# Positive part of the stick groups moved to ScalarE, and transposes copied before exponentials and masks in the dilated steps

## The reference

```python
# nsa_mixer: compressed, selected and window attention, softmax with slopes
# dilated_mixer: three groups of keys (distances up to 128, every 4th up to 512,
# every 16th up to 2048), softmax each, merged by their denominators
# stick_breaking_mixer:
z = jnp.einsum('bqhd,bshd->bhqs', qb, k).astype(jnp.float32) * scale
log_beta = jax.nn.log_sigmoid(z)
log_fail = jnp.where(causal, jax.nn.log_sigmoid(-z), 0.0)
after = lax.cumsum(log_fail, axis=3, reverse=True) - log_fail
a = jnp.where(causal, jnp.exp(log_beta + after), 0.0)
return jnp.einsum('bhqs,bshd->bqhd', a.astype(dt), v)
```

## Time and profile before

| what | value |
|---|---|
| median of 3 runs | 1158.55 us |
| profiled execution | 1152.53 us |
| its span | 1150.7 us |
| TensorE matmul busy | 1104.2 us (96%) |
| VectorE busy | 629.7 us (55%) |
| ScalarE busy | 423.9 us (37%) |
| GpSimd busy | 531.9 us (46%) |
| granted TensorE clock, mean | 0.99 |

### The profile page before, as it was taken

The page is one execution under the profiler, slowest core; times in us unless marked ns, Lnnn a source line. Parts: engine busy times, 40 slices in busy tenths (PEclk is TensorE's granted clock), DMA queues, the critical chain, the costliest instruction groups (busy, mean ns, idle before and its releaser), DMA issues.

```text
span 1150.7 us, 16133 instructions
## 1 busy us (share of the span) xinstructions
PE 1104.2 (96%) x5801; PEld 942.9 (82%) x5801; DVE 629.7 (55%) x1128; ACT 423.9 (37%) x852; POOL 531.9 (46%) x533
## 2 busy tenths in 40 slices
PE   6999999999989999999999987899999999999998
PEld 5788888888869888888798886788878888888887
DVE  6869786768556763656656577846531321321321
ACT  5374758363335551213464465523120200210210
POOL 0000000000442334979823567309976776777772
PEclk9999999999999999999999999899999999999999
DMA  6322322313220101333301200203322322232221
GB/s 250 125 96 83 119 91 92 128 55 125 95 73 19 38 20 37 111 105 116 127 21 55 73 2 2 72 1 110 128 92 95 103 96 92 97 104 91 91 91 54
DMA packets 27280, 97.18 MB, mean 84 GB/s; under 512 B 3024, under 2 KB 3408, under 8 KB 27088
## 3 DMA queue, kind: packets, MB, share of 16 engines
q1 hardware_dynamic: 27216, 96.32, 25.3%
HBM read 94.21 MB, written 2.10 MB: 84 GB/s over the span
## 4 chain that ended last, share of the span: by engine, by line
PE 73%; DVE 11%; issue 6%; ACT 5%; POOL 4%; DMA 1%; SPq 0%; POOLq 0%; DVEq 0%; ACTq 0%
PE bank L1276 21%; PE bank L1278 21%; PE bank L1277 20%; PE bank L788 4%; PE bank L751 3%; PE bank L768 2%; POOL wl L1229 1%; POOL wh L1226 1%; DVE arena L2006 1%; DVE wl L1957 1%; ACT wh L1637 1%; POOL wl L1228 1%; DVE arena L1025 1%; PE bank L810 1%; DMA x<-x_in 1%
## 5 line engine op out<-in xcount | busy, mean ns | idle before, releaser
L1225 POOL TENSOR_TENSOR hold<-hold 128x2 f32<-128x2 f32 x117 | 30.0, 257 | 519.4 <-PE bank L1278 519.4
L1276 PE MATMUL bank<-xh,wh 128*128 128x512 f32 x568 | 227.1, 400 | 11.4 <-DVE xl L1926 9.4
L1277 PE MATMUL bank<-xl,wh 128*128 128x512 f32 x568 | 222.6, 392 | 0.0
L1278 PE MATMUL bank<-xh,wl 128*128 128x512 f32 x568 | 222.5, 392 | 0.0
L1276 PE MATMUL bank<-yh,wh 128*128 128x512 f32 x520 | 203.4, 391 | 1.9 <-DVE yl L2346 1.5
L1278 PE MATMUL bank<-yh,wl 128*128 128x512 f32 x520 | 202.4, 389 | 0.0
L1277 PE MATMUL bank<-yl,wh 128*128 128x512 f32 x520 | 202.3, 389 | 0.0
L1229 POOL TENSOR_TENSOR wl<-raw,wh 128x512 fp32r<-128x512 f32 x117 | 174.3, 1490 | 0.0
L1228 POOL TENSOR_TENSOR wl<-raw,wh 128x512 fp32r<-128x512 f32 x117 | 157.9, 1349 | 9.8
L1276 PEld LDWEIGHTS bank<-xh,wh 128*128 128x128 f32 x568 | 107.6, 189 | 34.6 <-issue 11.6
L1226 POOL TENSOR_SCALAR wh<-raw 128x1024 fp32r<-128x1024 f32 x117 | 126.4, 1080 | 0.0
(11 more groups left out here) (257 smaller groups left out, 1804.7 us busy)
## 6 DMA issues: line engine op xcount, KB each, us to landing
raw<-weight_units SPq DMA_DIRECT2D x173, 512.0 KB, 3.5
x<-x_in SPq DMA_DIRECT2D x4, 512.0 KB, 8.1
out_fm<-x SPq DMA_DIRECT2D x8, 256.0 KB, 2.0
arena<-tables SPq DMA_DIRECT2D x1, 1024.0 KB, 10.1
par<-params SPq DMA_DIRECT2D x1, 166.0 KB, 2.3
arena<-swa_table SPq DMA_DIRECT2D x1, 128.0 KB, 11.1
ident<-identity SPq DMA_DIRECT2D x1, 64.0 KB, 9.2
```

Of the source, the lines that this page charges most:

```text
L1225: pool.tensor_tensor(hold[:], hold[:], hold[:], ALU.add).then_inc(held, 1)
L1276: pe.matmul(out, lh, rh, start=start, stop=False)
L1277: pe.matmul(out, lh, rl, start=False, stop=False)
L1278: return pe.matmul(out, ll, rh, start=False, stop=stop)
```

## The change

In attention 2 only:

1. Stick groups: ScalarE computes Relu(z) from the score bank into the probabilities' buffer `pr`, between Abs and Exp. The wait for the transposes of group i-4 goes with it from VectorE to ScalarE. VectorE's L1024 goes away; the scan adds both tensors, `pr` and the logarithm (add, add), and waits for a new semaphore `sparts` too.
2. A function `copies_first(i)` is true from step 56 on (when group i+4 is dilated or past the end). In these steps ScalarE and VectorE run `copy_out(i)` before `soft1(i+3)` and `mask1(i+3)`; on VectorE `finish` stays ahead of it, and `pair_out` and `divisors` come after. TensorE uses the same function for `late`, with the same order as before.

```diff
@@ make_attention
+            first_dilated = min((i for i, g in enumerate(groups) if batches[g["b"]]["kind"] == "dil"), default=None)
+            def copies_first(i):
+                return a == 2 and i + LOOK + 1 >= first_dilated
@@ pe_part
-                    late = ahead < ng and batches[groups[ahead]["b"]]["kind"] == "dil"
+                    late = copies_first(i)
...
-                    if late:
+                    if late and ahead < ng:
                         scores(ahead)
@@ act_part, soft1
                         act.activation(lt, score_bank(st)[:, 0:w], ACT.Abs).then_inc(s["soft1"], 1)
+                        if i >= 4:
+                            act.wait_ge(s["pt_ready"], groups[i - 4]["chunks"][-1][0] + 1)
+                        act.activation(pr[:, 0:w], score_bank(st)[:, 0:w], ACT.Relu).then_inc(s["sparts"], 1)
                         act.wait_ge(s["soft1"], n3 + 1)
                         act.activation(lt, lt, ACT.Exp, scale=-1.0).then_inc(s["soft1"], 1)
@@ act_part, steps
+                    if copies_first(i) and i < ng:
+                        copy_out(i)
                     if 0 <= i + LOOK < ng:
                         soft1(i + LOOK)
...
-                    if 0 <= i < ng:
+                    if 0 <= i < ng and not copies_first(i):
                         copy_out(i)
@@ dve_part, mask2
+                    dve.wait_ge(s["sparts"], stick_count(i) + 1)
                     dve.wait_ge(s["soft1"], 3 * stick_count(i) + 3)
-                    link(dve.scalar_tensor_tensor(out=lt, in0=z, scalar=0.0, in1=lt, op0=ALU.max, op1=ALU.add))
-                    link(dve.tensor_tensor_scan(lt[:, ::-1], ones[:, 0:1].to_broadcast([P, w]), lt[:, ::-1],
-                                                0.0, ALU.mult, ALU.add))
-                    if i >= 4:
-                        dve.wait_ge(s["pt_ready"], groups[i - 4]["chunks"][-1][0] + 1)
+                    link(dve.tensor_tensor_scan(lt[:, ::-1], pr[:, ::-1], lt[:, ::-1], 0.0, ALU.add, ALU.add))
                     dve.tensor_tensor(pr, z, lt, ALU.subtract).then_inc(strip_read(g["strip0"])[0], 1)
```

More of the change, by code:

```diff
@@ L420, in two_block_kernel @@
                 "scores", "read0_", "read1_", "read2_", "read3_", "soft1", "probs", "pt_ready", "pt_even", "pt_odd",
-                "o_done", "fin5_", "fin6_", "sprobs", "pairT", "pair_done", "esum")}
+                "o_done", "fin5_", "fin6_", "sprobs", "sparts", "pairT", "pair_done", "esum")}
         block = ctx.enter_context(nc.Block())
```

## The result

The changed kernel took 1162.61 us (median of 7 runs, 1160.61 to 1165.50) against 1156.96 us for the kernel before (7 runs, 1156.19 to 1159.84): ratio 1.0054, interval 1.0039 to 1.0070. It is slower by half a percent. 1158.0 was predicted, with 1152.0 to 1162.5 as range. The profiled execution took 1161.62 us, with a span of 1159.8 us against 1150.7 before. Of these 9.1 us of span some 3.5 say only that the profiled execution of before was one of its shortest (1152.53 us against its median of 1156.96); the medians are 5.7 apart.

What follows compares the result with a forecast made beforehand. TensorE, busy 96% of the span, was taken as the bound, so only its idle time in the second attention could be won. Sticks -2.8 plus dilated +2.2 gave -0.6 us against the 1158.55 median: 1158.0, range 1152.0 to 1162.5.

Steps and rivals of the forecast that it cites:

- The sticks: 24 stick groups: Relu onto ScalarE, L1024 off VectorE; eight stalls summed to a gain of 2.8 us, bounds 1.2 to 4.5.
- The scan at nothing: Stick groups: the scan reading two tensors and adding costs nothing extra; bounded between 0.42 and 1.85 us, 957 ns median.
- 723.45: TensorE's 1.09 us stall on the last stick subtraction, L1029, behind a 512-column group; gain 0.73 us.
- The dilated steps: Copies ahead of exponentials and masks from step 56: stalls shrink, but VectorE's masks come later; cost 2.2 us, ends 0.6 to 3.5.
- Step 57: First mask of group 60 comes 3.0 to 4.3 us after L1029 instead of 2.5; TensorE +0.5 to +1.8 us.
- Steps 60 and 61: The 1.50 us stall goes, VectorE's copy delays tables and masks of group 64; TensorE together at +1.2 us.
- Steps 62 and 63: The 1.11 us stall on VectorE's copy goes; TensorE at -0.15 us.
- Step 64: Copy goes ahead of group 67's masks and the pair's split, which comes about 1.9 us later; TensorE at +1.75 us.
- Step 65: Copy stands ahead of the second pair's split, for which transposes already waited 1.06 us; TensorE at +2.15 us.
- The clock: TensorE at half clock from 718 to 728 us; no gain given, forecast wrong if the level changes elsewhere.
- Rival 2: Slower: VectorE and TensorE in lockstep (+3.5), pair splits cost 1 us, Relu takes the stick gain back; 1163.0 us, chance 0.14.
- rival 1: Copies ahead in the dilated steps pay in full, -4.8 us, and sticks give 2.8; 1151.0 us, chance 0.23.

Runs made afterwards that it cites:

- old sticks: Changed kernel with the stick groups put back as before, both engines still copying first in the dilated steps; 1171.18 us, ratio 1.0118 to the kernel before.
- sticks only: Changed kernel with copies back behind exponentials and masks on both engines, so only the stick part is new; 1152.45 us, ratio 0.9959 to the kernel before.
- ten buffers: Changed kernel with ten buffers instead of four for the copied transposes of the dilated chunks; 1159.29 us, ratio 1.0032 to the kernel before.
- the six that mask first: Kernel before and the five follow-up kernels whose VectorE masks before copying from step 62 on; medians from 1148.91 to 1157.14 us.
- split ahead: Changed kernel with VectorE's split of the turned pair ahead of copy and masks in the dilated steps; 1160.06 us, ratio 1.0034 to the kernel before.
- both cures: Changed kernel with ten buffers for the dilated chunks and the pair's split ahead of the copy on VectorE; 1157.93 us, ratio 1.0008 to the kernel before.
- from step 62: Changed kernel, but VectorE copies first only from step 62 on and masks first in steps 56 to 61; 1159.55 us, ratio 1.0018 to the kernel before.
- filler: Changed kernel with 24 thrown-away transposes of the identity on TensorE ahead of a pair's transposes; 1163.47 us, ratio 1.0057 to the kernel before.

## Why the prediction was wrong

**The sticks: right sign, too small.** The forecast was -2.8 us, -1.2 to -4.5. In the two profiled executions the way from the first stick scores (559.52 before, 557.71 after) to the last scores of group 60 went from 163.93 to 161.58 us: -2.4. The comparisons that differ by the sticks alone say more: 0.9959 to 1 (-4.7 us), 1.0054 to 1.0118 (-7.4), 0.9918 to 0.9989 (-8.2). The traces explain the difference in part. In the other two kernels with the old sticks that way took 168.8 and 169.6 us, in ten of the eleven with the new ones 160.7 to 162.2 (165.5 in one); the profiled execution of before was one of its fastest. What made the others long is for the most part the clock. In the kernel with ScalarE's edit alone TensorE was busy 151.0 us on that way where it was 146.8 before, and idle 18.6 where it was 17.1; its clock from 602 to 720 us was 0.90, where the earlier trace rows has 0.96.

```profile
602.00:720.00 118.00, 106.19 (x677) 100.52 (x676) 72.75 (x197) 63.03 (x168) 64.55 (x71) 0.90 0.10 32
```

That the shorter chain is also what keeps the clock up there fits, but no run isolates it.

- The Relu cost what the Abs costs, as said: 259 to 607 ns against 258 to 599, no table load.

```profile
L870 ACT ACTIVATE arena<-bank x24: 259/442/607, 559.4 to 714.3; 128x128 f32<-128x128 f32 x6, 128x256 f32<-128x256 f32 x6, 128x384 f32<-128x384 f32 x6, 128x512 f32<-128x512 f32 x6
L1036 DVE TENSOR_TENSOR_SCAN arena<-arena x24: 418/958/2293, 560.3 to 716.2; 128x128 f32<-128x128 f32 x6, 128x256 f32<-128x256 f32 x6, 128x384 f32<-128x384 f32 x6, 128x512 f32<-128x512 f32 x6
```

- ScalarE's later copies were covered, as said: TensorE's waits for L930 are 3.6 us where L919 had 3.3, those for L910 2.6 where L901 had 4.0.
- The Trainium skill, "ScalarE: Activation LUTs", "Rules for kernel authors", puts relu on VectorE, not on ScalarE. The rows here don't bear it out: at 512 columns of fp32 from a bank the Relu took ScalarE 607 ns, where VectorE took 692 for the maximum with its addition and 692 for a plain copy. No run has the Relu alone on VectorE. That the kernel with this edit alone is 0.4% faster speaks for moving work off the engine that is late, not for either engine's speed.
- The scan at nothing: right in the median (958 against 957 ns), too low at its longest (2.29 us, outside my bound of 1.85). The scans that now start earlier ended no earlier where GpSimd was at work; that is the next point and the last section.
- The stalls came out otherwise one by one than in the sum. 697.46 was to lose 0.72 and did (1.18 to 0.46). 716.80 was to lose 0.16 and lost 1.2 (1.48 to 0.30), and 0.75 us at 606.66, which the forecast did not list, went. But 609.78 was to lose 0.46 and grew from 1.26 to 1.95. And 570.00, where L1024 "stood in that chain with no slack" for a gain of 0.45, stayed at 1.69: the scan started 0.47 us earlier, counted from the first stick scores, and took 1.18 us for 256 columns instead of 0.73.

```profile
566.38 1.18 DVE L1036 TENSOR_TENSOR_SCAN arena<-arena 128x256 f32<-128x256 f32 x1
568.16 0.30 PE L757 MATMUL bank<-yh 128*128 128x128 f32 x1 [1.69 <-DVE arena L1037]
```

- 723.45 was to lose 0.73 and grew from 1.09 to 2.50 at 719.29. TensorE came earlier, the scan did not end earlier; see the last section. The Relu is not what lengthened it: in the two other traces with the old sticks the same wait is 2.50 and 2.51 us.

**The dilated steps: the term that failed.** Forecast +2.2 (0.6 to 3.5). Measured +13.2 between the traces, 11.0 us by the ratios of the changed kernel and "sticks only" (1.0054 to 0.9959). The forecast's numbers by step say how late TensorE stands there against before, so they are not to be added; the last one, 2.15, is the 2.2. The same count from the traces, from the last scores of group 60 on, gives 1.4 to 1.8 us behind step 57's wait, 2.5 behind step 61's, 5.4 at the values of group 63, 9.7 at the pair's transposes of step 64, 11.2 at the transposes of step 65 and 13.2 at the end. By steps:

- Step 57: the first mask was to cost TensorE 0.5 to 1.8 us. The trace has a wait of 2.17 us for it at 723.14, and by the places of the instructions that both traces have TensorE stood 1.4 to 1.8 us late behind it. Right.
- Steps 60 and 61: the 1.50 us wait of the earlier trace rows went, as said, and 2.00 us for the mask came at 736.38. Mechanism right; TensorE stood 2.5 us late behind it, not 1.2.
- Steps 62 and 63: forecast -0.15. The 1.11 us wait went, as said. But the copy of 746.91 waited for a buffer (2.33), the masks came late, and 0.64 us of waiting stands at 747.73. The rest of the way from 2.5 to 5.4 us late is the clock.
- **Step 64 is the step that failed**: "The masks start at 749.05 instead of 747.13 ... +1.75". They started at 752.68 (TensorE stood 1.2 us behind its time of before by then), because I let the copy start when its transposes were done and forgot its second wait, for the buffer. It is in the code (`earlier` in the copy) and in the trace of before. The wait came to 4.22 us. The run with ten buffers tells the two parts apart: without the buffer's wait 2.00 us were left, near the 1.9 by which the forecast had moved the split, so 2.2 us are the forgotten wait. I had asked what each moved instruction costs, not what all its waits are.
- Step 65: forecast 0.4 us later than step 64. The wait grew by 1.1 us, from 1.06 to 2.16, and TensorE stood 1.5 us later than at step 64, the clock included.
- **The clock**: I gave it nothing, neither way, and said that it would be wrong if it changed its level elsewhere. It did: 6.7 us of the 13.2. In the middle before had 4.8 us at half clock; the changed kernel had 6.8 from 720.4 and 6.8 from 737.5. In the tail before had none; the changed kernel had 10.2 from 754.5. The tail's share came in and behind waits which the order of copies made; for the middle that is open, as "sticks only" shows.

The sum of the waits was thus some three times too low, and the other half was not in the sum. Rival 2 had the right sign and nearly the right time (1163.0 against 1162.6), and that is luck in part. The lockstep held, and the first tables did stay beside GpSimd at half clock (2.15 us at 720.60). But the Relu took nothing back, and the splits cost through what stood before them. The rival had the dilated steps at 4.5 us, where the ratios give 11.0, and the sticks at 0, where they give -4.7; these two errors nearly cancel, and its starting point of 1158.55 us, 1.6 above the median measured beside the result, took up the rest.

Of rival 1 the half on ScalarE came true in its mechanism and not in its price. There the copy ahead takes away the 1.50 us wait and costs nothing, but waits for VectorE of 1.54 us (alone) and 1.21 us (with the sticks, 0.50 and 0.71) stand in its place. That fits the ratio of 0.9989 alone. The 0.4% with the sticks is the middle: 25.04 us instead of 28.10, of which TensorE's busy time is 22.13 instead of 25.35, so it is the clock and not the wait. Whether the edit brings that about, or its pair met the clock once well and once badly, stays open; with ten buffers the same kernel stands at 0.9957, no better than sticks only.

## What to carry to other kernels

Before an instruction is moved to the head of an in-order queue, list every wait it carries, the one for its destination buffer too, and then everything behind it whose reader is idle by then: a wait that was free at the end of a step brought 2.2 of the 4.2 us that TensorE waited once it stood in front of one. The same edit cost nothing on ScalarE, with exponentials behind it, and 13.7 us on VectorE (by the medians), with masks that free the score banks and a pair's split behind it; so make such an edit engine by engine. And where TensorE's waits grow, allow for matmuls at the lower clock, here as much again as the waits, and don't take one profiled execution for the kernel: the first one shown was 4.4 us below its median.

## What the runs showed of the hardware

**In the tail the half clock went with the waits; in the middle it is less plain.** Within the middle and tail the granted clock had only the levels 1.0 and 0.5 (2.4 and 1.2 GHz). In the changed kernel it was at 0.5 from 720.4 and from 737.5 for 6.8 us each and from 754.5 for 10.2 us; in the kernel with ScalarE's edit alone on top of the sticks, with no wait over 1.11 us after 735 us, it was never at 0.5 from there to the end of the tail. The second of these stretches began 1.1 us behind the end of a wait of 2.00 us (736.38). In it TensorE was never idle:

```profile
737.50:744.20 6.70, 6.70 (x31) 6.60 (x30) 2.33 (x8) 3.17 (x13) 0.00 (x0) 0.50 0.02 4
```

So TensorE worked for 6.7 us without a pause at the lower level. In the tail waits and half clock went together in every trace:

| kernels | TensorE's waits of over 0.5 us in the tail | at half clock, us |
|---|---|---|
| the six that mask first | at most 1.07 | 0 |
| split ahead | 3.53 | 3.4 |
| both cures | 2.90 | 3.4 |
| ten buffers | 2.00 and 2.16 | 6.8 |
| changed, old sticks, from step 62 | 4.22 and 2.16 | 10.2 |
| filler | 1.50 and 2.16 | 10.2 |

(In the kernel in which only VectorE copies first it was 17.1 us, with waits of 2.41, 4.21 and 2.16.) The middle does not follow so well. "Sticks only" had the waits of before there, 1.50 and 1.11 us, and was at half clock for 3.4 us from 734.6 and again from 744.8, where before was at full clock. So the waits alone don't decide it, and what else does no run shows.

**A scan waits for GpSimd.** The scan in front of the wait of 2.50 us (VectorE, then GpSimd):

```profile
716.22 2.29 DVE L1036 TENSOR_TENSOR_SCAN arena<-arena 128x512 f32<-128x512 f32 x1 [0.21 <-ACT arena L874]
```

```profile
716.15 1.28 POOL L1239 TENSOR_TENSOR wl<-raw,wh 128x512 fp32r<-128x512 f32 x1
```

It began 0.07 us behind GpSimd's subtraction, which ended at 717.43, and ended itself 1.08 us after that. Scans of 512 columns with no GpSimd instruction beside them took 1.22 or 1.23 us in both traces (four before, five after). GpSimd in turn waited for the scan: its next instruction, about 0.2 us long in most other places, took 1.12 and ended at 718.50, with the scan (718.51):

```profile
717.38 1.12 POOL L1235 TENSOR_TENSOR hold<-hold 128x2 f32<-128x2 f32 x1
```

Before, the scan of the same group began at 721.28, 0.31 us ahead of the end of such a subtraction, and ended 1.09 us behind it. So both ended the same time after GpSimd, and the time that VectorE had won by losing L1024 was gone again: that is where the gain expected at 723.45 went. One kernel, with the sticks, ScalarE's copies first and ten buffers, met GpSimd otherwise. There the scan of this group began 0.01 us ahead of a subtraction and took 1.23 us, the subtraction took 2.28, and the wait behind the scan was 1.38 us instead of 2.50:

```profile
718.70 1.23 DVE L1048 TENSOR_TENSOR_SCAN arena<-arena 128x512 f32<-128x512 f32 x1 [0.16 <-ACT arena L886]
718.71 2.28 POOL L1248 TENSOR_TENSOR wl<-raw,wh 128x512 fp32r<-128x512 f32 x1
720.71 0.45 PE L769 MATMUL bank<-xh 128*128 128x128 f32 x2 [1.38 <-DVE arena L1049]
```

The Trainium skill, "SBUF — State Buffer", section "SBUF: two separate sides", says that a VectorE operation with two inputs in SBUF and a GpSimd operation that reads SBUF hold a shared pair of ports in turn, each for its whole length; all three pairs of rows agree with it.
